# Query projection tiles loaded into gather buffers before the gathers, the first eight expert picks chosen alone, single rows at the end, token tiles loaded first

## Chip, core and metric

One core of one Trainium2 chip runs the whole program. The metric is the device time of one execution in microseconds. Three runs of the kernel before gave 1580.16, 1581.84 and 1583.11 us; their median is 1581.84 us.

## What is computed

Two model blocks run one after the other on 256 tokens of width 1024 (272 rows with the 16 meta rows in the first mixer). The first block is a hybrid mixer followed by a product-key expert layer (PEER). The second block is a retention layer and a stick-breaking attention layer. The change touches the beginning of the first block and its expert layer:

```python
hn = rmsnorm(h, ln_mix_w)                      # h = meta rows and token rows, 272 x 1024
h  = h + hybrid_mixer(hn, ...)                 # ends with  mixed @ w_out
...
q = (hn @ w_q).reshape(n, 8, 2, 128)           # query projection, w_q is 1024 x 2048
s = einsum('nhid,hikd->nhik', q, sub_keys)     # 8 heads x 2 sides x 128 keys
s_top, i_top = top_k(s, 16)                    # per side
cand = s_top[..., 0, :, None] + s_top[..., 1, None, :]
best, pos = top_k(cand, 16)                    # 16 of 256 pairs
idx = key 0 * 128 + key 1 of each pick         # row of the expert tables
w = softmax(best)
act = gelu(einsum('nhkd,nd->nhk', u_tab[idx], hn))
out = einsum('nhk,nhkd->nd', w * act, v_tab[idx])
```

Each token picks 8 x 16 = 128 expert rows, each a row of u and a row of v, 2 x 1024 floats.

## The kernel before

**Weight stream.** All dense weights come as 257 tiles of 128 x 1024 floats (512 KB) in one fixed order, `chunks`. Tile i is loaded by SP (L201) into `raw[i % 4]` by `load` (L210), is split by `do_split` (L215) into a high part (`whi`, ACT, L221) and a low part (`wlo`, DVE, L222) in a ring of five, and is multiplied in three matmuls per product by `triple` (L260). `next_chunk` (L227) splits tile i + 4 when tile i is taken, and each split issues the load of the tile four further on, so a raw buffer is filled again as soon as its split is done. I call the 16 tiles of `peer_w_q` w_q0 to w_q15, and the first tiles after them (retention weights) ret0 to ret3. The output projection takes the eight tiles before w_q0.

**Order by hand.** Each engine runs its own list in program order. Only waits on semaphores tie the lists together. `stream_T` and `stream_N` emit the matmuls of a tile and then one step of a generator in `sides` (`side_step`), so the expert layer's DVE work is laid between the splits: one step of `peer_side` (L1230) after each w_q tile from w_q2 on, and freely once the tiles are out.

**Expert layer.** A pair n = (head, half of the tokens) has 16 picks. `topk(n)` (L1121) finds them on DVE in steps: best 16 of side 0, best 16 of side 1, best 16 of the 256 sums, the table rows (L1134 to L1141), the softmax weights. `gather(m)` (L1176) issues one indirect DMA on POOL (L1187) which brings row m's u and v for 128 tokens, 1 MB, into one of 17 slots; m runs from 0 to 255. Slots 0 to 6 are in the arena AR, 7 and 8 at the upper end of the XH and XL halves of SLAB, 9 is the key table SUBK, 10 to 14 are the `whi`/`wlo` ring and 15 and 16 the rest of XH and XL. `slot_free` (L1159) says what each must wait for on first use: slots 0 to 8 for the output projection, slot 9 for the last scores, slots 10 to 16 for matmuls of the last w_q tiles. Later uses wait for the expert matmul that read the slot's former row. `slot_for` takes the slot that has been held longest.

**Per row.** `dot(m)` (L1196, DVE) multiplies u with HN, the weighted rows made by `weighted_rows` (L1045). `gelu` (L1205, ACT) follows for a group of 4 rows, of 2 from m = 228, of 1 from m = 254. For a group of several, one DVE product (L1210) and a diagonal per row on ACT (L1222); for a single row, one DVE instruction makes the diagonal (L1220). `expert(m)` then does two matmuls with v (L323). The first group's product and matmuls come in the list after dot(10), when the last w_q tile and its scores are out. At m = 243, 245, ... `peer_side` also splits ret0 to ret3.

**Start.** SP loads token tile 0, then the meta rows, which wait until DVE has zeroed their 128 x 1024 tile, then token tile 1, constants C1, parameters PAR and the first four raw tiles. Token tile 1 and the meta rows share a semaphore. Sums of squares (L380 to L382) and `rstd` follow; then per quarter of the width the rows are scaled: meta and tile 0 on DVE (L388, L389), tile 1 on ACT (L390). TensorE transposes them (L326), waiting for C1 and PAR, and L333/L334 split them into XH and XL.

Of the kernel before, what the change touches and what calls it, by code (L numbers as in the profile page):

```python
# [143 lines left out]
def build(nc, stream, par, rows, con1, con2, xin, meta, subk, peer_uv, out, stage=99, debug=None):  # L144
    chunks = chunk_plan()
    ctx = ExitStack()
    with ctx:
# [62 lines left out]
        def load(i):  # L210
            if i < len(chunks) and i == state["load"]:
                state["load"] += 1
                loaded[i] = dma(SP, raw[i % NR][:, :], stream[i], s_raw[i % NR], split.get(i - NR), state["hold"])

        def do_split(i):  # L215

            if i < min(len(chunks), state["limit"]) and i == state["split"]:
# [1641 lines left out]
```

How the kernel before makes its waits and increments, by code:

```python
    def run(self, eng):  # L73
        for waits, make, signal in self.program:
            for sem, value in waits:
                eng.wait_ge(sem, value)
            ins = make(eng)
            if signal:
                ins.then_inc(self.sem, 1)
# [64 lines left out]
def build(nc, stream, par, rows, con1, con2, xin, meta, subk, peer_uv, out, stage=99, debug=None):  # L144
# [55 lines left out]
            def make(e, dst=dst, src=src, s=s):  # L200
                return e.dma_start(dst, src).then_inc(s, 16)
# [974 lines left out]
        def gather(m):  # L1176
# [8 lines left out]
            s = s_uv[j]  # L1185
            dma_count[s.name] = dma_count.get(s.name, 0) + 16
            G(lambda e: e.indirect_dma_start(slots[j], None, peer_uv, bass.IndirectOffsetOnAxis(ap=col, axis=0)).then_inc(s, 16),
              idx_pt[m // 16], free, signal=False, chain=False)
# [535 lines left out]
        A(lambda e: e.activation(SM[:, 30:31], SM[:, 30:31], ACT.Sqrt))  # L1724
        YY = place("YY", 8704, 2048).rearrange("p (i d) -> p i d", i=2)
        stream_N(2, 16, 0, TX, 0, sb_ready, use_y, pick=sb_pick)
        OUT = place("OUT", 10752, 2048).rearrange("p (i d) -> p i d", i=2)
        row_rstd()
        v = post(OUT, False)
        s_out = sem("s_out")
        for (half, i), t in v.items():
            f = slice(512 * half, 512 * half + 512)
            done = dma(SP, out[128 * i:128 * i + 128, f], OUT[:, i, f], s_out, t)
        SP(lambda e: e.wait_ge(*done), signal=False)
        return finish(locals())
```

## Time and profile before

| | us |
|---|---|
| median of three runs | 1581.84 |
| the profiled execution's own time | 1588.28 |
| its span, first to last instruction | 1586.5 |
| PE busy | 1382.9 (87%) |
| PE weight load busy | 992.7 (63%) |
| DVE busy | 1086.4 (68%) |
| ACT busy | 720.7 (45%) |
| POOL busy | 298.5 (19%) |
| mean granted TensorE clock | 0.959 |

The shares are means over stages with different limits. The dense stages (to about 480 us, and from about 1145 us) are filled by PE. Between them lies the expert stage, which moves 268 MB of gathered rows. Times within the span are counted from its first instruction. "Releaser" is what ended an engine's idle time.

### The profile page before, as it was taken

The numbers are of one execution on the slowest core, as the hardware profiler recorded it, in microseconds if no ns is written. First come the engines' busy times: TensorE is split into PE (matmuls) and PEld (weight loads), VectorE is DVE, ScalarE is ACT, GpSimd is POOL, SyncE is SP. The second block draws the span as 40 slices with busy tenths as digits, with TensorE's granted clock in tenths as the row PEclk, the third lists the DMA queues.
The fourth block names the chain that finished last, engine by engine and source line by source line (L and its number), as shares of the span: only waits on it lengthen the run. The fifth ranks groups of instructions, "written<-read, shape, count | busy, mean of one in ns | idle before, by whom it ended". The sixth has DMA issues, their size and how long they took to land. (4 is left out here: it accounts for less than half of the span.)

```text
span 1586.5 us, 19019 instructions
## 1 busy us (share of the span) xinstructions
PE 1382.9 (87%) x6585; PEld 992.7 (63%) x6585; DVE 1086.4 (68%) x2076; ACT 720.7 (45%) x1242; POOL 298.5 (19%) x260
## 2 busy tenths in 40 slices
PE   6999989989999787777877777788799999999997
PEld 5989978968988333333333333333397788998776
DVE  5778578676678777777777677665686466765554
ACT  5666677556454222222222222222454365657772
POOL 0000000000004554443544444442100000000000
PEclk9999999999999898998989999989999999999999
DMA  6453444444559999999999999999655456445442
GB/s 229 125 183 120 161 147 146 140 126 155 178 173 380 418 422 421 421 421 421 422 421 421 422 420 422 421 420 422 271 191 162 124 183 198 158 162 145 147 135 78
DMA packets 77808, 417.73 MB, mean 263 GB/s; under 512 B 8768, under 2 KB 8832, under 8 KB 44688
## 3 DMA queue, kind: packets, MB, share of 16 engines
q0 software_dynamic: 36864, 268.45, 40.7%
q1 hardware_dynamic: 40848, 148.06, 29.4%
q8 instruction: 53, 0.87, 0.2%
q14 instruction: 43, 0.35, 0.1%
HBM read 415.39 MB, written 1.08 MB: 263 GB/s over the span
## 5 line engine op out<-in xcount | busy, mean ns | idle before, releaser
L323 PE MATMUL ps<-AR 128*128 128x512 f32 (+6 forms) x1164 | 365.0, 463 | 103.1 <-ACT AR L1222 74.1
L222 DVE TENSOR_TENSOR wlo<-raw,whi 128x1024 fp32r<-128x1024 f32 x257 | 312.0, 1220 | 159.9 <-ACT whi L221 159.3
L323 PEld LDWEIGHTS ps<-AR 128*128 128x128 f32 (+2 forms) x1164 | 188.9, 194 | 266.6 <-issue 126.6
L221 ACT ACTIVATE whi<-raw 128x1024 fp32r<-128x1024 f32 x257 | 269.2, 1054 | 118.7 <-PE ps L260 95.6
L260 PE MATMUL ps<-XH,whi 128*128 128x256 f32 (+1 forms) x1032 | 305.3, 296 | 9.4 <-DVE XL L334 2.5
L323 PE MATMUL ps<-SLAB,AR 128*128 128x512 f32 x516 | 248.9, 637 | 62.6 <-ACT AR L1222 62.5
L260 PE MATMUL ps<-XL,whi 128*128 128x256 f32 (+1 forms) x1032 | 296.4, 287 | 0.0
L260 PE MATMUL ps<-XH,wlo 128*128 128x256 f32 (+1 forms) x1032 | 296.4, 287 | 0.0
L1187 POOL DMA_INDIRECT AR<-in_peer_uv,C x127 | 148.2, 1167 | 650.0 <-DVE C L1141 475.2
L323 PEld LDWEIGHTS ps<-SLAB,AR 128*128 128x128 f32 x516 | 102.9, 204 | 206.3 <-issue 121.1
L260 PEld LDWEIGHTS ps<-XH,whi 128*128 128x128 f32 x1032 | 199.9, 194 | 19.2 <-issue 6.1
L1196 DVE CUSTOM_DVE_ANT_0 SLAB<-SLAB,AR 128x1024 f32<-128x1024 f32 x129 | 156.8, 1222 | 63.7 <-DMA SLAB<-in_peer_uv,C 63.6
L260 PEld LDWEIGHTS ps<-XL,whi 128*128 128x128 f32 x1032 | 199.9, 194 | 0.7 <-issue 0.5
L260 PEld LDWEIGHTS ps<-XH,wlo 128*128 128x128 f32 x1032 | 199.7, 194 | 0.0
L1196 DVE CUSTOM_DVE_ANT_0 AR<-AR 128x1024 f32<-128x1024 f32 x127 | 154.3, 1222 | 55.2 <-DMA AR<-in_peer_uv,C 54.8
L260 PE MATMUL ps<-whi,XH 128*128 128x512 f32 x448 | 184.9, 413 | 0.0
L1187 POOL DMA_INDIRECT SLAB<-in_peer_uv,C x129 | 150.2, 1164 | 173.8 <-PE ps L323 132.3
L260 PE MATMUL ps<-whi,XL 128*128 128x512 f32 x448 | 176.3, 393 | 0.0
L260 PE MATMUL ps<-wlo,XH 128*128 128x512 f32 x448 | 176.2, 393 | 0.0
L1222 ACT ACTIVATE AR<-C 128x128 f32<-128x128 f32 x254 | 84.4, 392 | 177.3 <-DVE C L1210 150.4
L1205 ACT ACTIVATE C<-C,SM 128x4 f32<-128x4 f32 (+2 forms) x72 | 21.4, 297 | 290.0 <-DVE C L1196 289.8
L260 PEld LDWEIGHTS ps<-whi,XH 128*128 128x128 f32 x448 | 85.2, 190 | 19.5 <-issue 3.2
(251 smaller groups left out, 1219.4 us busy)
## 6 DMA issues: line engine op xcount, KB each, us to landing
raw<-in_stream SPq DMA_DIRECT2D x257, 512.0 KB, 3.9
AR<-scr SPq DMA_DIRECT2D x8, 512.0 KB, 5.4
SLAB<-in_peer_uv,C POOLq DMA_INDIRECT x129, 28.1
AR<-in_rows SPq DMA_DIRECT2D x4, 512.0 KB, 4.7
AR<-in_peer_uv,C POOLq DMA_INDIRECT x127, 27.9
AR<-in_con SPq DMA_DIRECT2D x1, 1280.0 KB, 7.1
AR<-in_xin SPq DMA_DIRECT2D x2, 512.0 KB, 4.9
AR<-in_xin SPq DMA_DIRECT2D x1, 1024.0 KB, 6.1
```

What stands on the lines that cost most here:

```text
L221: a = A(lambda e: e.activation(h[:, :], r, ACT.Copy), loaded[i], free, chain=False)
L222: b = V(lambda e: e.tensor_tensor(l[:, :], r, h[:, :].bitcast(F32), ALU.subtract), a, loaded[i], free, chain=False)
L260: tok = PE(lambda e, s=s, m=m, n=n: e.matmul(out_ap, s, m, start=first and n == 0, stop=last and n == 2), *(after if n == 0 else ()), sign ...
L323: return PE(lambda e: e.matmul(out_ap, l, r, start=start, stop=stop, skip_group_check=onto), *after, signal=sig)
L1187: G(lambda e: e.indirect_dma_start(slots[j], None, peer_uv, bass.IndirectOffsetOnAxis(ap=col, axis=0)).then_inc(s, 16), idx_pt[m // 16], f ...
L1196: dot_pt[m] = V(lambda e: e.tensor_tensor_reduce(u, u, HN[:, i, :], 1.0, 0.0, ALU.mult, ALU.add, AV[:, i, at:at + 1]), uv_in[m], chain=False)
L1205: gelu_pt[ms[0]] = A(lambda e: e.activation(CC[:, i, c], AV[:, i, c], ACT.Gelu_apprx_tanh, scale=SM[:, 24 + i:25 + i]), dot_pt[ms[-1]])
L1222: a = A(lambda e: e.activation(d, ident, ACT.Copy, scale=CC[:, i, c]), c_ready, dg_free.get(m - 4), chain=False)
```

## The change

There are four edits. (1) Eleven of the w_q tiles, w_q4 to w_q14, no longer pass through the four raw buffers. They get homes of their own in gather slots 0, 1, 4, 5, 7 and 8; each is loaded on a semaphore of its own once the matmuls of the SSD up projection (`yt_done`) are over. One of these loads is issued after each split. The raw ring holds the other tiles, so the load which w_q0's split issues is that of w_q15, and the splits of w_q1 to w_q3 issue ret0 to ret2. A slot with a lent tile is offered to `gather` only when the tile's split has been emitted, and waits for it; slot 6, which needs HN, only when HN has been. (2) `topk(0)` finds its best eight pairs, makes their table rows, and only then the other eight. The first gathers are issued between the two, ahead of `weighted_rows`. (3) Groups of one row begin at m = 248 instead of 254. (4) At the start the meta tile is zeroed on POOL, token tile 1 is loaded ahead of the meta rows, with semaphores of their own, and the meta rows are scaled on POOL.

```diff
-        def load(i):
-            if i < len(chunks) and i == state["load"]:
+        first_pq = next(n for n, c in enumerate(chunks) if c[1] == "peer_w_q")
+        high = 2 * NS * CH + 8 * T
+        spare = [(0, AR, 4096), (0, AR, 5120), (4, AR, 20992), (4, AR, 22016), (5, AR, 23040), (5, AR, 24064), (1, AR, 14848),
+                 (7, SLAB, high), (7, SLAB, high + CH), (8, SLAB, high + XW), (8, SLAB, high + XW + CH)]
+        extra = {first_pq + NR + n: buf[:, at:at + CH] for n, (_, buf, at) in enumerate(spare)}
...
+        in_ring = [i for i in range(len(chunks)) if i not in extra]
+        ring_at = {i: n for n, i in enumerate(in_ring)}
+        pending = []
+
+        def load(n):
+            if n < len(in_ring) and n == state["load"]:
...
-                r, h, l = raw[i % NR][:, :], whi[i % NS], wlo[i % NS]
+                r, h, l = extra[i] if i in extra else raw[ring_at[i] % NR][:, :], whi[i % NS], wlo[i % NS]
...
-                load(i + NR)
+                if i in ring_at:
+                    load(ring_at[i] + NR)
+                if pending:
+                    pending.pop(0)()
+
+        def load_ahead(ready):
+
+            for i, tile in extra.items():
+                def make(i=i, tile=tile):
+                    loaded[i] = dma(SP, tile, stream[i], sem(f"s_extra{i}"), ready)
+                pending.append(make)
...
-        z0 = V(lambda e: e.memset(HX[:, 2, :], 0.0))
+        m0 = G(lambda e: e.memset(HX[:, 2, :], 0.0))
         x0_in = dma(SP, HX[:, 0, :], x_tiles[:, 0, :], s_x)
         s_x1 = sem("s_x1")
-        x1_in = dma(SP, HX[0:16, 2, :], meta, s_x1, z0)
+        s_m = sem("s_m")
         x1_in = dma(SP, HX[:, 1, :], x_tiles[:, 1, :], s_x1)
+        meta_in = dma(SP, HX[0:16, 2, :], meta, s_m, m0)
...
-                V(lambda e, f=f: e.tensor_scalar(HX[0:16, 2, f], HX[0:16, 2, f], ss[0:16, 2:3], None, ALU.mult))
+                g = G(lambda e, f=f: e.tensor_scalar(HX[0:16, 2, f], HX[0:16, 2, f], ss[0:16, 2:3], None, ALU.mult), r)
...
-                ready = (ready[1], (v, a)) if c else (None, (v, a))
+                ready = (ready[1], (v, a, g)) if c else (None, (v, a, g))
...
         yt_done = PE.now()
+        load_ahead(yt_done)
...
+            if n == 0:
+                V(lambda e: e.max(BV[:, 0:8], CAND))
+                V(lambda e: e.max_index(idx[:, 0:8], BV[:, 0:8], CAND))
+                early["idx"] = pairs(slice(0, 8))
+                yield
+                V(lambda e: e.match_replace(CAND, BV[:, 0:8], CAND, NEG))
+                V(lambda e: e.max(BV[:, 8:16], CAND))
+                V(lambda e: e.max_index(idx[:, 8:16], BV[:, 8:16], CAND))
+                v = V(lambda e: e.tensor_scalar(SM[:, 28:29], BV[:, 0:1], -1.0, None, ALU.mult))
+                idx_pt[n] = pairs(slice(8, 16))
...
+            if j == 6 and "hn" not in pts:
+                return None
             if j < EARLY:
-                return (pts["hn"], wo_done) if j == 6 else (pts["r"], wo_done, yt_done)
+                tiles = [split.get(i) for i in lent.get(j, ())]
+                if None in tiles:
+                    return None
+                return (pts["hn"], wo_done) if j == 6 else (pts["r"], wo_done, yt_done, tiles)
...
-              idx_pt[m // 16], free, signal=False, chain=False)
+              early["idx"] if m < 8 else idx_pt[m // 16], free, signal=False, chain=False)
...
-            for _ in range(3):
+            for _ in range(2):
                 next(first_topk)
-            weighted_rows()
...
+            while m_next < 8 and gather(m_next):
+                m_next += 1
+            next(first_topk)
+            weighted_rows()
             gathers()
...
-                size = 4 if m < 228 else 2 if m < 254 else 1
+                size = 4 if m < 228 else 2 if m < 248 else 1
```

`pairs(c)` is the former run of seven instructions L1134 to L1141, applied to the picks in the slice c.

## Rows read from the trace of the kernel before

**Rows 1.** Page, part 2: GB/s moved by DMA, in 40 slices of the span.
```profile
GB/s 229 125 183 120 161 147 146 140 126 155 178 173 380 418 422 421 421 421 421 422 421 421 422 420 422 421 420 422 271 191 162 124 183 198 158 162 145 147 135 78
```

**Rows 2.** Windows: stretch, length, five engines' busy us, PE clock, DMA share, GB/s.
```profile
900.00:1080.00 180.00, 137.96 (x279) 57.23 (x280) 126.79 (x307) 40.84 (x107) 79.21 (x69) 0.91 1.01 421
...
534.00:535.00 1.00, 1.00 (x3) 0.40 (x3) 0.00 (x0) 0.40 (x1) 0.31 (x1) 1.00 0.86 295
```

**Rows 3.** Timeline of POOL: start, us, instruction, idle time before it and releaser.
```profile
475.60 2.00 POOL L1187 DMA_INDIRECT AR<-in_peer_uv,C  x1 [475.16 <-DVE C L1141]
...
490.65 0.94 POOL L1187 DMA_INDIRECT SLAB<-in_peer_uv,C  x1 [0.30 <-issue]
506.50 1.10 POOL L1187 DMA_INDIRECT SLAB<-in_peer_uv,C  x1 [14.91 <-PE ps L260]
...
521.35 1.72 POOL L1187 DMA_INDIRECT AR<-in_peer_uv,C  x1 [0.31 <-DVE SM L1131]
531.26 1.36 POOL L1187 DMA_INDIRECT AR<-in_peer_uv,C  x1 [8.19 <-PE ps L323]
```

**Rows 4.** DMA issues from 475.5 to 512 us: count, size, median us to landing.
```profile
raw<-in_stream SPq DMA_DIRECT2D x9, 512.0 KB, 11.9
```

**Rows 5.** Timeline of DVE around the first picks and up to the first group's product.
```profile
469.18 0.43 DVE L1128 TENSOR_TENSOR AR<-AR 128x256 f32<-128x256 f32 x1
...
470.18 0.42 DVE L1116 FIND_INDEX8 AR<-AR 128x8 uint32<-128x256 f32 x1
...
472.34 0.17 DVE L1134 TENSOR_SCALAR AR<-AR 128x16 uint32<-128x16 uint32 x1
...
473.69 0.69 DVE L1139 TENSOR_TENSOR AR<-AR 128x512 f32<-128x512 f32 x1
...
475.14 0.18 DVE L1141 SCALAR_TENSOR_TENSOR C<-AR 128x16 uint32<-128x16 f32 x1
...
477.83 4.62 DVE L222 TENSOR_TENSOR wlo<-raw,whi 128x1024 fp32r<-128x1024 f32 x4
...
488.31 1.23 DVE L222 TENSOR_TENSOR wlo<-raw,whi 128x1024 fp32r<-128x1024 f32 x1 [4.18 <-ACT whi L221]
...
526.70 0.16 DVE L1210 TENSOR_TENSOR C<-C 128x4 f32<-128x4 f32 x1
```

**Rows 6.** Timeline of ACT: the split of w_q11.
```profile
487.22 1.06 ACT L221 ACTIVATE whi<-raw 128x1024 fp32r<-128x1024 f32 x1 [4.59 <-DMA raw<-in_stream]
```

**Rows 7.** Timeline of PE: the first expert matmuls.
```profile
527.35 7.92 PE L323 MATMUL ps<-AR 128*128 128x512 f32 x14 [10.21 <-ACT AR L1222]
```

**Rows 8.** Windows before the gathers, columns as in Rows 2.
```profile
440.00:444.00 4.00, 4.00 (x19) 3.25 (x18) 2.51 (x3) 1.73 (x3) 0.00 (x0) 1.00 0.97 365
...
472.00:476.00 4.00, 4.00 (x36) 4.00 (x35) 3.62 (x10) 2.28 (x4) 0.40 (x1) 1.00 0.01 4
```

**Rows 9.** Landing time of the one raw load issued at 442.6 us (w_q3).
```profile
DMA to landing us min/median/max: 4.6/4.6/4.6
```

**Rows 10.** Timelines of PE and DVE: the last expert rows.
```profile
1137.33 5.42 PE L323 MATMUL ps<-AR 128*128 128x512 f32 x12 [1.25 <-ACT AR L1222]
1142.59 1.88 PE L323 MATMUL ps<-SLAB,AR 128*128 128x512 f32 x4
...
1139.15 1.22 DVE L1196 CUSTOM_DVE_ANT_0 SLAB<-SLAB,AR 128x1024 f32<-128x1024 f32 x1 [0.45 <-DMA SLAB<-in_peer_uv,C]
...
1140.75 0.34 DVE L1220 TENSOR_SCALAR AR<-C 128x128 f32<-128x128 f32 x1 [0.36 <-ACT C L1205]
```

**Rows 11.** Timelines of DVE and PE at the start, and landing of PAR's load issued at 3.3 us.
```profile
1.02 0.91 DVE L365 MEMSET AR<- 128x1024 f32 x1 [1.02 <-PEq L1849]
...
8.25 1.22 DVE L382 CUSTOM_DVE_ANT_0 AR<-AR 128x1024 f32<-128x1024 f32 x1 [5.66 <-DMA AR<-in_xin]
...
11.81 2.82 PE L326 MATMUL ps<-C,AR 128*128 128x128 f32 x12 [11.81 <-DVE AR L389]
...
DMA to landing us min/median/max: 7.9/7.9/7.9
```

More of the change, by code:

```diff
@@ L208, in build @@
         state = {"load": 0, "split": 0, "next": 0, "limit": PEER_END, "fence": None, "hold": None}
-        def load(i):
-            if i < len(chunks) and i == state["load"]:
+        first_pq = next(n for n, c in enumerate(chunks) if c[1] == "peer_w_q")
[3 more added lines that the diff above has]
+        extra = {first_pq + NR + n: buf[:, at:at + CH] for n, (_, buf, at) in enumerate(spare)}
+        lent = {}
+        for n, (j, _, _) in enumerate(spare):
+            lent.setdefault(j, []).append(first_pq + NR + n)
+        in_ring = [i for i in range(len(chunks)) if i not in extra]
[3 more added lines that the diff above has]
+            if n < len(in_ring) and n == state["load"]:
                 state["load"] += 1
-                loaded[i] = dma(SP, raw[i % NR][:, :], stream[i], s_raw[i % NR], split.get(i - NR), state["hold"])
+                i = in_ring[n]
+                loaded[i] = dma(SP, raw[n % NR][:, :], stream[i], s_raw[n % NR], split.get(in_ring[n - NR]) if n >= NR else None,
+                                state["hold"])
         def do_split(i):
@@ L380, in build @@
         a = A(lambda e: e.activation(junk[:, 0, :], HX[:, 0, :], ACT.Square, accum_out=ss[:, 0:1]), x0_in, z0)
-        a = A(lambda e: e.activation(junk[0:16, 0, :], HX[0:16, 2, :], ACT.Square, accum_out=ss[0:16, 2:3]), x1_in)
+        a = A(lambda e: e.activation(junk[0:16, 0, :], HX[0:16, 2, :], ACT.Square, accum_out=ss[0:16, 2:3]), meta_in)
         V(lambda e: e.tensor_tensor_reduce(junk[:, 1, :], HX[:, 1, :], HX[:, 1, :], 1.0, 0.0, ALU.mult, ALU.add, ss[:, 1:2]), x1_in)
@@ L1111, in build @@
         iota16 = C1[:, C_IOTA:C_IOTA + 16]
-        idx_pt, w_pt, c_pt = {}, {}, {}
+        idx_pt, w_pt, c_pt, early = {}, {}, {}, {}
         def best16(vals, idx, src):
@@ L1136, in topk, with pairs @@
-            V(lambda e: e.tensor_copy(AF, AB.bitcast(U32)))
-            V(lambda e: e.tensor_tensor(EQ, AF.unsqueeze(3).broadcast_to([128, 2, 16, 16]),
-                                        iota16.unsqueeze(1).unsqueeze(1).broadcast_to([128, 2, 16, 16]), ALU.is_equal))
-            V(lambda e: e.tensor_tensor(EQ, EQ, TF.unsqueeze(2).broadcast_to([128, 2, 16, 16]), ALU.mult))
-            V(lambda e: e.tensor_reduce(SEL, EQ, AX.X, ALU.add))
-            idx_pt[n] = V(lambda e: e.scalar_tensor_tensor(IDX[:, i, 16 * h:16 * h + 16], SEL[:, 0, :], 128.0, SEL[:, 1, :], ALU.mult,
-                                                           ALU.add))
+            def pairs(c):
+                m = c.stop - c.start
+                eq = EQ[:, :, c, :]
+                V(lambda e: e.tensor_single_scalar(AB[:, 0, c].bitcast(U32), BI[:, c].bitcast(U32), 4, ALU.logical_shift_right))
+                V(lambda e: e.tensor_single_scalar(AB[:, 1, c].bitcast(U32), BI[:, c].bitcast(U32), 15, ALU.bitwise_and))
+                V(lambda e: e.tensor_copy(AF[:, :, c], AB[:, :, c].bitcast(U32)))
+                V(lambda e: e.tensor_tensor(eq, AF[:, :, c].unsqueeze(3).broadcast_to([128, 2, m, 16]),
+                                            iota16.unsqueeze(1).unsqueeze(1).broadcast_to([128, 2, m, 16]), ALU.is_equal))
+                V(lambda e: e.tensor_tensor(eq, eq, TF.unsqueeze(2).broadcast_to([128, 2, m, 16]), ALU.mult))
+                V(lambda e: e.tensor_reduce(SEL[:, :, c], eq, AX.X, ALU.add))
+                return V(lambda e: e.scalar_tensor_tensor(IDX[:, i, 16 * h + c.start:16 * h + c.stop], SEL[:, 0, c], 128.0, SEL[:, 1, c],
+                                                          ALU.mult, ALU.add))
@@ new lines, in topk @@
+            idx = BI.bitcast(U32)
+            if n == 0:
[8 more added lines that the diff above has]
+                idx_pt[n] = pairs(slice(8, 16))
+            else:
+                best16(BV, idx, CAND)
+                v = V(lambda e: e.tensor_scalar(SM[:, 28:29], BV[:, 0:1], -1.0, None, ALU.mult))
+                yield
+                idx_pt[n] = pairs(slice(0, 16))
```

5 lines of the change are left out of this document (removed).

## Prediction

> **What bounds the kernel now.** I read the page's slices first, then windows, then the timelines of the expert stage. The slices show DMA at 421 GB/s from about 480 us to 1110 us and at 120 to 230 GB/s in nearly all other slices [rows 1]. In the windows PE, DVE, ACT and POOL are each well under full while the DMA share is 1.01 [rows 2]. So the expert stage runs at the pace of the transfers, and one gather of 1.049 MB costs 1.049 / 0.421 = 2.49 us. The dense stages on both sides are paced by PE. A us saved ahead of the expert stage, or at its end, comes off the total.
>
> The first reading would be that DMA is the bound from the first gather on, so that every byte taken out of the stage is a gain. POOL's timeline says otherwise. There are 17 slots. The first gather is issued at 475.6 us, the ninth at 490.65, the tenth at 506.5, the 17th at 521.35, and the 18th only at 531.26, after 8.2 us in which POOL waited for an expert matmul [rows 3]. The 18th needs a used slot. Its packets follow its issue by about 2.7 us, so they start near 534. In the window from 534 to 535 us the rate falls to 295 GB/s [rows 2]: the 17 gathers and the loads beside them are just used up then. From there the other 239 gathers run without a gap until the last one lands at 1139.15 us [rows 10], (1139.15 - 534) / 239 = 2.53 us each. The end of the expert stage is the time of the 18th gather plus a fixed 605 us. What counts is what releases the 18th gather.
>
> That is a chain on DVE. The 18th gather waits for expert row 0 on PE, whose matmuls start at 527.35 [rows 7], these for the diagonals on ACT, and these for the first group's product on DVE at 526.70 [rows 5]. In program order this product stands behind the splits of w_q11 to w_q15, dots 0 to 10 and the steps of topk(1) to topk(3). From 488.31 to 526.70 us DVE's timeline has no idle time worth counting. Ahead of it is one hole: the split of w_q11 waits 4.18 us for ACT [rows 5], and ACT waits 4.59 us for w_q11's load [rows 6], which was issued at 479.1, after the first gather.
>
> **Part 1, the tiles loaded ahead.** Nine raw loads (w_q11 to w_q15, ret0 to ret3) are issued between 475.5 and 512 us [rows 4]. In the new order eight of them (all but ret3) are issued before the first gather. That is 8 x 0.524 = 4.19 MB, or 10.0 us of transfer. Only what was waited for comes back: the hole of 4.18 us on DVE. On PE more is saved, since ACT no longer holds up copies behind its waits for loads, but PE is idle for 10.2 us before 527.35 [rows 7], so that saving ends in a longer idle. Value: -4.2 us.
>
> What it adds: gathers 4 to 8 must wait for splits in their slots. Stepping through the lists, gathers 0 to 3 find slots 0, 2, 3 and 6. Gathers 4 to 6 wait on POOL for w_q10's split (about 484 us), gather 7 for w_q12's (about 491), gather 8 for w_q14's (about 501), with gathers 9 and on queued behind it. DMA then runs dry between about 497 and 504 us, and again for some 3 us before the 18th gather. It costs nothing while dots find their rows: dot 8 comes about 12 us after gather 8 is issued, dot 10 about 19 us after gather 10. I take 0, with a bound of 2 us should a row land late.
>
> The doubled loads fall into the output projection: from 436 to 455 us one ring tile and one lent tile per split, 1.05 MB in about 2.8 us or 374 GB/s, against 421 possible. The stretch is not idle now: 365 GB/s from 440 to 444 us, falling to 4 GB/s at 472 to 476 [rows 8]. Behind the key table's load the raw loads would land at intervals of 1.25 us, alternating: w_q3, issued at 442.6, lands after 4.6 us now [rows 9], and with four lent tiles ahead of it at about 447.1 + 3 x 1.25 = 450.9. ACT splits it at 452.2. The smallest slack is about 1.3 us, at w_q2 and w_q3, so I take 0. It is a rival below.
>
> **Part 2, eight picks first.** The seven instructions from 472.34 to 475.32 take 2.98 us; their three long ones take 0.69 each at 512 columns, and 0.43 at 256 columns [rows 5]. For eight picks they take 2.98 - 3 x 0.26 = 2.2 us, and twice that is 4.4, so DVE pays 1.42 us more ahead of HN, the splits of w_q7 to w_q10 and all that follows. The first gather gains: the first index search ends at 470.6, + 2.2 = 472.8, issue at 473.1 instead of 475.6. But an earlier first gather only fills slots sooner; it doesn't move the DVE chain. So this part costs 1.4 us. With part 1 the chain moves by -4.2 + 1.4 = **-2.8 us** (-2.2 to -3.2; 2 us less if a row lands late). PE's w_q7 would wait some 0.1 us for its low part.
>
> **Part 3, single rows from m = 248.** Now rows 252 and 253 wait for each other, PE starts row 252 at 1137.33 and works off four rows to 1144.3 at 1.72 us each [rows 10], though row 255's diagonal is ready at 1141.1. Singly, row 252's dot (ends 1133.0) lets PE start it at 1134.1, row 253 at 1137.0 (a split stands ahead of its diagonal), row 254 at 1139.1 and row 255 at 1141.1, ending at 1142.9. The price on DVE is a wait for gelu of 0.36 and a diagonal of 0.34 per row [rows 10], so two rows with a split take 4.8 us of the 4.98 in which they land. Value: **-1.4 us** (0 to -1.6).
>
> **Part 4, the start.** Token tile 1 lands at 8.2 us [rows 11], 5.9 us after its issue at 2.4. Issued at 1.2 right behind tile 0, which lands at 4.7, it should land at about 6.5. The scaled rows would then be ready 1.7 us sooner, at about 10.0. But the transposes need PAR too, which lands at 3.3 + 7.9 = 11.2, against their start at 11.81 [rows 11]. PAR gains only what the gap in the transfers gives back, up to 0.8 us. So the transposes start 0.6 to 1.4 us earlier, and DVE, rid of four scalings of 0.34 us, gives some 0.4 on the way to the last transpose. POOL's zeroing and scaling are not in the trace (POOL shows no such instruction). DVE takes 0.91 us to zero the tile [rows 11], and from it I bound POOL's between 0.9 and 3 us; at 3 us the meta rows' load, with constants, PAR and raw tiles queued behind it on SP, goes out 1.5 us later, and the gain becomes a loss of about 0.5. Value: **-1.6 us** (+0.5 to -2.3). The Trainium skill (GPSIMD Engine Reference, § 4.1 Engine selection) speaks against the move in general, calling elementwise work on GpSimd about twice as slow with two inputs, but roughly line rate with one; both moved operations have one, and by that rule the sum stays. No run yet shows it.
>
> **Sum.** -2.8 - 1.4 - 1.6 = **-5.8 us**. The profiled execution took 1588.28 us (span 1586.5), 6.4 us above the median of the runs, so it would take 1582.5, and the median goes from 1581.84 to **1576.0 us**. The terms' bounds reach from 1574.7 to 1580.1.
>
> **Rivals.** (a) *The bytes come back one for one.* If DMA and not the chain releases the stage, its saturated stretch loses 10.0 us and starts 2.5 us earlier: 1581.84 - 10.0 - 2.5 - 1.4 - 1.6 = 1566.3 us. For it speaks the full DMA share; against it the 18th gather's wait for PE and the dip at 534. Chance 0.08. The Trainium skill (DMA: Bandwidth & Descriptors, § Queues, rings and completion order) says that each DMA engine takes turns between the queues that have work, so loads and gathers share the rate, which would favour this case; the trace agrees on the sharing (raw loads land after 11.9 us in that stretch [rows 4]), not on what limits the stage.
>
> (b) *Start and tail give nothing, or a row lands late.* POOL is slow or PAR holds the start, and DVE's gelu waits eat the tail's gain, or gather 8's wait holds up dot 8: what is left is about -2.8 us, 1579.0, within 0.2%. Chance 0.20.
>
> (c) *Slower: the doubled loads starve the projections.* If the loads between 436 and 455 us move slower than 374 GB/s, each pair puts the next ring tile later. PE then waits in the output projection and at w_q0 to w_q3, and all behind it is late. It decides once a tile has lost its 1.3 us of slack; at one tile time of 1.25 us for each of eight pairs it costs 10 us: 1576.0 + 10.0 = 1586.0. For it speaks 365 GB/s already at 440 to 444 us [rows 8]; against it, the expert stage's rate of 421. Chance 0.06.
>
> **How the numbers follow.** Forecast 0.66, (a) 0.08, (b) 0.20, (c) 0.06. A measurement of this kernel can tell about 0.2%, or 3.2 us. The forecast's bounds up to 1578.7 are faster by more than that, as is (a), and a quarter of (b): faster 0.79; the rest of (b) within: 0.15; slower 0.06. The range takes in the forecast's bounds and most of (b), and reaches toward (a): 1570.5 to 1580.5.
>
> **What would show it.** Part 1: no wait of ACT for a load in the w_q stage, w_q11's split on DVE right behind dot 0 and its softmax step, no raw load but ret3's between the first gather and 512 us; POOL waiting for ACT or DVE splits before gathers 4, 7 and 8; DMA below full near 500 us. The first group's product 2.8 us nearer to the start of the w_q stage than now, the 18th gather likewise, and the same 605 us after it. Part 2: the first gather 2.5 us earlier against that stage, HN 1.4 us later. Part 3: L1220 eight times, PE's end 3.8 us after the last landing instead of 5.2. Part 4: the first transposes at about 10.5, the first product 1.6 us earlier. It is wrong if the 18th gather follows the transfers and not the first product, or if PE idles between 436 and 460 us.

## The result, and the profile after

| | before | after |
|---|---|---|
| median of five runs, one chip | 1581.99 us | 1575.83 us |
| their range | 1580.16 to 1583.77 | 1574.50 to 1577.61 |
| ratio with 95% interval | | 0.9952 [0.9939, 0.9965] |
| the profiled execution's own time | 1588.28 | 1575.83 |
| its span | 1586.5 | 1574.0 |
| mean granted TensorE clock | 0.959 | 0.964 |

The kernel is faster by 6.2 us or 0.48% (interval 0.35 to 0.61%). It was forecast at 1576.0 us with a gain of 5.8 us. Two rows of the page of after, the engines' one and that of rows 1:

```profile
PE 1377.8 (88%) x6585; PEld 986.6 (63%) x6585; DVE 1086.9 (69%) x2081; ACT 719.0 (46%) x1239; POOL 302.6 (19%) x265
GB/s 231 130 179 121 161 148 139 156 135 161 188 289 324 399 421 420 422 422 421 421 421 421 422 421 422 421 421 421 262 193 165 130 184 193 158 162 145 149 135 80
```

The two profiled executions differ by more than the medians: 12.5 us of span. That has to be sorted out first, or each term would be read too large. The landmark is the first copy out of PSUM at the start of the w_q stage, on ACT; I call it w. From before and then from after, ACT's timeline, and one window of each in the mixer stage (columns as in rows 2):

```profile
461.28 0.37 ACT L1081 COPY AR<-ps 128x256 f32<-128x256 f32 x1
300.00:350.00 50.00, 45.46 (x217) 35.29 (x216) 32.85 (x41) 26.01 (x44) 0.00 (x0) 0.93 0.43 137
```
```profile
454.38 0.37 ACT L1107 COPY AR<-ps 128x256 f32<-128x256 f32 x1
300.00:350.00 50.00, 47.12 (x243) 37.67 (x244) 36.34 (x45) 28.14 (x46) 0.00 (x0) 1.00 0.49 157
```

From the first product to w, a stretch in which only loads were added, before took 461.28 - 19.91 = 441.4 us and after 454.38 - 18.02 = 436.4. The window shows what goes with it: the granted clock was 0.93 in before and 1.00 in after, though the matmuls of the stage are the same. Other profiles speak against an effect of the change. `short_before` below has the code of before in this stretch and took 435.2 us; a second profile of after took 439.7. So 5.0 of the 12.5 us are set aside: what lies ahead of the mixer stage is read from the span's start, and everything behind it is counted from w.

POOL's timeline of after, to be held against rows 3: gathers 1, 4, 5, 8, 9 and 18.

```profile
466.18 1.15 POOL L1236 DMA_INDIRECT AR<-in_peer_uv,C  x1 [452.53 <-ACT AR L1088]
...
472.69 1.68 POOL L1236 DMA_INDIRECT AR<-in_peer_uv,C  x1 [2.71 <-DVE AR L1071]
477.73 1.18 POOL L1236 DMA_INDIRECT AR<-in_peer_uv,C  x1 [3.37 <-ACT AR L1107]
...
484.71 1.17 POOL L1236 DMA_INDIRECT SLAB<-in_peer_uv,C  x1 [2.88 <-DVE wlo L236]
494.57 1.17 POOL L1236 DMA_INDIRECT SLAB<-in_peer_uv,C  x1 [8.69 <-ACT AR L1088]
...
521.64 1.22 POOL L1236 DMA_INDIRECT AR<-in_peer_uv,C  x1 [11.43 <-PE ps L347]
```

DVE's timeline of after, to be held against rows 5: both instructions of `weighted_rows`, the splits of w_q7 to w_q10, the softmax step after dot 0, w_q11's split, and the first group's product.

```profile
469.94 2.49 DVE L1071 TENSOR_TENSOR AR<-AR 128x1024 f32<-128x1024 f32 x2
472.34 4.62 DVE L236 TENSOR_TENSOR wlo<-AR,whi 128x1024 fp32r<-128x1024 f32 x4
...
478.41 0.23 DVE L1190 TENSOR_SCALAR C<-C,SM 128x16 f32<-128x16 f32 x1
478.55 1.22 DVE L236 TENSOR_TENSOR wlo<-SLAB,whi 128x1024 fp32r<-128x1024 f32 x1
...
516.94 0.16 DVE L1259 TENSOR_TENSOR C<-C 128x4 f32<-128x4 f32 x1
```

The hole of 4.18 us in front of w_q11's split [rows 5] is gone: the split starts at 478.55 directly behind the softmax step, with no idle time noted. The first group's product comes 516.94 - 454.38 = 62.6 us after w, where before had 526.70 - 461.28 = 65.4. The 18th gather still waits for an expert matmul, now for 11.43 us.

The transfers of after, in windows with the columns of rows 2:

```profile
492.00:496.00 4.00, 4.00 (x36) 4.00 (x35) 3.83 (x10) 3.10 (x7) 1.17 (x1) 1.00 0.00 2
...
508.00:512.00 4.00, 0.00 (x0) 0.00 (x0) 3.72 (x14) 0.00 (x0) 1.91 (x2) 0.50 1.02 424
...
522.00:523.00 1.00, 1.00 (x3) 0.47 (x2) 0.96 (x4) 0.40 (x1) 0.86 (x1) 0.50 0.28 115
523.00:524.00 1.00, 1.00 (x3) 0.40 (x2) 0.40 (x2) 0.00 (x0) 0.00 (x0) 0.79 0.86 123
524.00:525.00 1.00, 1.00 (x4) 0.52 (x3) 0.00 (x0) 0.40 (x1) 0.56 (x1) 1.00 0.55 180
```

They fall to 2 GB/s while the ninth gather waits for its slot, run at 424 again, and dip just before the 18th gather's packets arrive. I call the size of that dip D. It is the time that the transfers lose against 421 GB/s in the 20 us from 8 us ahead of the 18th gather's issue to 12 us behind it: 20 x (421 - rate) / 421. These windows of before, of after and of `lent7`, an experiment below:

```profile
523.26:543.26 20.00, 15.91 (x33) 7.02 (x34) 10.98 (x23) 7.87 (x18) 8.27 (x7) 0.81 1.01 416
```
```profile
513.64:533.64 20.00, 16.05 (x31) 7.08 (x32) 10.05 (x22) 7.65 (x17) 7.00 (x7) 0.76 0.94 375
```
```profile
513.60:533.60 20.00, 15.81 (x33) 7.01 (x34) 11.07 (x23) 7.86 (x18) 8.41 (x7) 0.82 0.83 323
```

D is 2.2 us in after, 4.7 in lent7, and only 0.2 in before, where the window of 295 GB/s [rows 2] is the one low one and some of its neighbours lie above 421. The depth of this dip will matter more than anything else below.

The tail, PE's and DVE's timelines of after, to be held against rows 10:

```profile
1130.68 1.98 PE L347 MATMUL ps<-SLAB,AR 128*128 128x512 f32 x4 [0.20 <-DVE AR L1269]
1132.50 1.94 PE L350 MATMUL ps<-C,AR 128*128 128x128 f32 x16
...
1128.68 1.23 DVE L1245 CUSTOM_DVE_ANT_0 SLAB<-SLAB,AR 128x1024 f32<-128x1024 f32 x1 [0.24 <-DMA SLAB<-in_peer_uv,C]
...
1130.28 0.35 DVE L1269 TENSOR_SCALAR AR<-C 128x128 f32<-128x128 f32 x1 [0.36 <-ACT C L1254]
```

The transposes that follow the last row start 3.8 us after the last landing, against 5.2 us in before, from 1139.15 [rows 10] to this row of its PE timeline:

```profile
1144.31 1.94 PE L326 MATMUL ps<-C,AR 128*128 128x128 f32 x16
```

Without the mixer stage the profiled difference is 7.5 us: 1.9 at the start, 3.6 from w to the last landing, 1.3 in the tail and 0.7 behind it. The medians say 6.2.

### The profile page after: what moved, and what is told of

The parts are those of the page before. It is cut to its first block and busy times, and to the rows that moved or that the text cites. A ratio compares the mean times of both kernels' runs of the same rounds, so it can differ in the third digit from the quotient of the medians.

```text
span 1574.0 us, 19025 instructions
## 1 busy us (share of the span) xinstructions
PE 1377.8 (88%) x6585; PEld 986.6 (63%) x6585; DVE 1086.9 (69%) x2081; ACT 719.0 (46%) x1239; POOL 302.6 (19%) x265
## 3 DMA queue, kind: packets, MB, share of 16 engines
HBM read 415.39 MB, written 1.08 MB: 265 GB/s over the span
## 5 line engine op out<-in xcount | busy, mean ns | idle before, releaser
L347 PE MATMUL ps<-AR 128*128 128x512 f32 (+6 forms) x1164 | 369.2, 466 | 98.1 <-ACT AR L1271 71.6
L236 DVE TENSOR_TENSOR wlo<-raw,whi 128x1024 fp32r<-128x1024 f32 x246 | 298.6, 1221 | 150.5 <-ACT whi L235 149.8
L235 ACT ACTIVATE whi<-raw 128x1024 fp32r<-128x1024 f32 x246 | 257.5, 1054 | 100.7 <-PE ps L284 90.3
L347 PE MATMUL ps<-SLAB,AR 128*128 128x512 f32 x516 | 244.0, 627 | 62.1 <-ACT AR L1271 61.9
```

The costliest lines, as they stand in the source:

```text
L235: a = A(lambda e: e.activation(h[:, :], r, ACT.Copy), loaded[i], free, chain=False)
L236: b = V(lambda e: e.tensor_tensor(l[:, :], r, h[:, :].bitcast(F32), ALU.subtract), a, loaded[i], free, chain=False)
L347: return PE(lambda e: e.matmul(out_ap, l, r, start=start, stop=stop, skip_group_check=onto), *after, signal=sig)
```

## The experiments

Two theories stood against each other. The chain theory: the 18th gather follows DVE's chain, and the bytes taken out of the gather stage are worth nothing by themselves. The transfer theory, rival (a): the stage takes as long as its bytes, and each 421 KB are worth 1 us. The table gives for each profile, in us, P (the first group's product), G (the 18th gather's issue) and L (the last landing, by the start of the last dot), all counted from w, then L - G and D; then the median and the ratio to the kernel before in the same session. Lines with the same session number share a chip and its runs of before.

| kernel | P | G | L | L - G | D | median, us | ratio to before | session |
|---|---|---|---|---|---|---|---|---|
| before | 65.4 | 70.0 | 677.9 | 607.9 | 0.2 | 1581.99 | 1 | 0 |
| after | 62.6 | 67.3 | 674.3 | 607.0 | 2.2 | 1575.83 | 0.9952 [0.9939, 0.9965] | 0 |
| no_lent | 67.1 | 71.8 | 679.4 | 607.6 | 1.5 | 1579.86 | 0.9985 [0.9974, 0.9996] | 1 |
| no_early8 | 61.5 | 66.2 | 674.0 | 607.8 | 2.8 | 1572.94 | 0.9951 [0.9936, 0.9966] | 1 |
| no_tail | 62.6 | 66.9 | 674.6 | 607.6 | 2.6 | 1579.06 | 0.9977 [0.9967, 0.9987] | 1 |
| no_start | 62.9 | 67.6 | 674.7 | 607.2 | 2.5 | 1577.84 | 0.9969 [0.9957, 0.9980] | 1 |
| short_before | 60.2 | 64.9 | 677.8 | 612.9 | 0 | 1581.14 | 0.9992 [0.9980, 1.0004] | 2 |
| short_after | 56.2 | 60.9 | 672.1 | 611.2 | 0 | 1573.90 | 0.9943 [0.9925, 0.9961] | 2 |
| bytes_back | 63.5 | 68.2 | 675.8 | 607.6 | 0.7 | 1578.39 | 0.9960 [0.9946, 0.9974] | 2 |
| lent7_short | 56.2 | 60.9 | 669.8 | 608.9 | 0 | 1571.53 | 0.9925 [0.9907, 0.9942] | 2 |
| after_again | 62.5 | 66.8 | 674.5 | 607.7 | 2.4 | 1574.68 | 0.9960 [0.9946, 0.9974] | 3 |
| lent7 | 62.5 | 67.0 | 674.7 | 607.7 | 4.7 | 1575.21 | 0.9957 [0.9945, 0.9969] | 3 |
| lent7_short_again | 56.2 | 60.9 | 670.0 | 609.2 | 0 | 1571.26 | 0.9926 [0.9912, 0.9941] | 3 |

P repeats within 0.1 us in two profiles of one kernel (62.56 and 62.54; 56.19 and 56.15), G and L within 0.4. That is far finer than the medians, so the marks carry the argument and the ratios check it.

**Undo part 1 (no_lent).** No tile is lent, all else as in after.

```diff
-        spare = [(0, AR, 4096), (0, AR, 5120), (4, AR, 20992), (4, AR, 22016), (5, AR, 23040), (5, AR, 24064), (1, AR, 14848),
-                 (7, SLAB, high), (7, SLAB, high + CH), (8, SLAB, high + XW), (8, SLAB, high + XW + CH)]
+        spare = []
```

> The changed kernel without its first part: no tile has a home in a gather slot, all pass through the four raw buffers again. Chain theory (the 18th gather follows the first group's product on DVE): the hole before w_q11's split is back, 4 to 5.5 us, so the first product comes 4 to 5.5 us later against the w_q stage than in the changed kernel, and the time is about 1576 + 5 = 1581 us, 1 us below the kernel before, since start and tail still give 3.2 us and the second part costs DVE 1.4 us. Bytes theory (the transfers set the end of the expert stage): 10 us of loads are back in the stage, 1576 + 10 = 1586 us.

ACT's and DVE's timelines of no_lent, w_q11's split on both:

```profile
484.96 1.06 ACT L234 ACTIVATE whi<-raw 128x1024 fp32r<-128x1024 f32 x1 [5.34 <-DMA raw<-in_stream]
...
486.05 1.23 DVE L235 TENSOR_TENSOR wlo<-raw,whi 128x1024 fp32r<-128x1024 f32 x1 [4.30 <-ACT whi L234]
```

The hole is back with its cause: ACT waits for the load, DVE for ACT. P is 4.6 us later than in after, G 4.6, L 5.1. The time loses most of the change's gain: 0.9985 against 0.9952. Where the transfer theory wanted 1586 us, it is 1579.86. This kernel also gives the price of part 2 under the old chain: P is 67.1 - 65.4 = 1.7 us later than in before.

**Undo part 2 (no_early8).** `topk(0)` runs through as in before, `weighted_rows()` and the gathers follow.

```diff
-            if n == 0:
+            if n < 0:
...
-              early["idx"] if m < 8 else idx_pt[m // 16], free, signal=False, chain=False)
+              idx_pt[m // 16], free, signal=False, chain=False)
...
-            for _ in range(2):
+            for _ in range(3):
                 next(first_topk)
+            weighted_rows()
...
-            while m_next < 8 and gather(m_next):
-                m_next += 1
-            next(first_topk)
-            weighted_rows()
             gathers()
```

> The changed kernel without its second part: topk(0) chooses all 16 picks at once and the gathers come behind HN. Chain theory: DVE is spared 1.4 us ahead of the w_q7 split, so the first product and the 18th gather come 1.4 us earlier and the time is 1576 - 1.4 = 1574.6 us, although the first gather is issued 2.5 us later. Theory that the first gather sets the stage: 1576 + 2.5 = 1578.5 us.

P moved by 1.1 us and G by 0.7 to 1.1, but L by only 0.3 against after and 0.6 against after_again, and the ratio stayed (0.9951). The first gather was issued 14.3 us behind w instead of 11.8. So the part costs 1.1 to 1.7 us in the chain, as its instructions say. How much of that reaches the end stays open between 0.3 and 1: L scatters by 0.4 between profiles and the ratios by more. The earlier first gather has bought nothing visible: undone, D is 2.8, not smaller than the 2.2 of after.

**Undo part 3 (no_tail).**

```diff
-                size = 4 if m < 228 else 2 if m < 248 else 1
+                size = 4 if m < 228 else 2 if m < 254 else 1
```

> The changed kernel with groups of two rows up to m = 253 again. If the tail gave what the prediction says: PE ends its last expert row 5.2 us after the last landing instead of 3.8, and the time is 1576 + 1.4 = 1577.4 us. Rival (DVE's waits for gelu ate it): no change, 1576 us.

PE's and DVE's timelines of no_tail, the end of the gather stage:

```profile
1129.92 5.42 PE L347 MATMUL ps<-AR 128*128 128x512 f32 x12 [1.24 <-ACT AR L1271]
...
1131.74 1.23 DVE L1245 CUSTOM_DVE_ANT_0 SLAB<-SLAB,AR 128x1024 f32<-128x1024 f32 x1 [0.44 <-DMA SLAB<-in_peer_uv,C]
...
1136.90 0.27 PE L350 MATMUL ps<-C,AR 128*128 128x128 f32 x1
```

PE again works off 12 matmuls in one piece while the last row is already there; the transposes start at 1136.90, 5.2 us behind the landing. The mark says 1.34 us. The ratio is 0.0025 above that of after, 4 us, with intervals of 0.0010 and 0.0013 to either side, and 0.0017 above that of after_again; it confirms the sign and is too coarse for the size.

**Undo part 4 (no_start).**

```diff
-        m0 = G(lambda e: e.memset(HX[:, 2, :], 0.0))
+        z0 = V(lambda e: e.memset(HX[:, 2, :], 0.0))
...
+        x1_in = dma(SP, HX[0:16, 2, :], meta, s_x1, z0)
         x1_in = dma(SP, HX[:, 1, :], x_tiles[:, 1, :], s_x1)
-        meta_in = dma(SP, HX[0:16, 2, :], meta, s_m, m0)
...
-        a = A(lambda e: e.activation(junk[0:16, 0, :], HX[0:16, 2, :], ACT.Square, accum_out=ss[0:16, 2:3]), meta_in)
+        a = A(lambda e: e.activation(junk[0:16, 0, :], HX[0:16, 2, :], ACT.Square, accum_out=ss[0:16, 2:3]), x1_in)
...
-                g = G(lambda e, f=f: e.tensor_scalar(HX[0:16, 2, f], HX[0:16, 2, f], ss[0:16, 2:3], None, ALU.mult), r)
+                V(lambda e, f=f: e.tensor_scalar(HX[0:16, 2, f], HX[0:16, 2, f], ss[0:16, 2:3], None, ALU.mult))
...
-                ready = (ready[1], (v, a, g)) if c else (None, (v, a, g))
+                ready = (ready[1], (v, a)) if c else (None, (v, a))
```

> The changed kernel with the start of the kernel before: the meta tile zeroed on DVE, meta rows loaded ahead of token tile 1, meta rows scaled on DVE. If the start gave what the prediction says, the first product of the first stage comes at 19.9 us instead of 18.0 and the time is 1576 + 1.9 = 1577.9 us. Rival (the start is covered by the loads of the first weight tiles): no change, 1576 us.

The first product, PE's timeline of no_start and then of after:

```profile
19.86 0.57 PE L284 MATMUL ps<-XH,whi 128*128 128x272 f32 x1
```
```profile
18.02 0.37 PE L284 MATMUL ps<-XH,whi 128*128 128x272 f32 x1
```

They are 1.84 us apart. But the old start is not the same each time. From PE's timelines, the first transposes of short_before (whose start is before's), and of after:

```profile
10.89 2.82 PE L326 MATMUL ps<-C,AR 128*128 128x128 f32 x12 [10.89 <-DVE AR L389]
```
```profile
10.89 2.79 PE L350 MATMUL ps<-C,AR 128*128 128x128 f32 x12 [10.89 <-POOL AR L413]
```

In short_before token tile 1 happened to land at 7.3 us instead of 8.2, and the first transposes then start at 10.89, as in after. Its first product still came at 18.98, 1.0 us later than in after. The three profiles with the old start give 19.91, 19.86 and 18.98 us, the ten with the new one (after among them) 17.8 to 18.4. By this mark the part is worth 1.5 to 2.1 us in the usual case and 0.6 to 1.2 when the old order is lucky. After is one of four profiles in which the mark came 0.6 us early for another reason; part 4 below takes that apart.

**Is it the bytes? (bytes_back).** After, with eight transfers of 512 KB added in the gather stage, one behind each of the splits of w_q7 to w_q14. They copy weight tiles to a scratch tensor that nobody reads, so the 4.19 MB that part 1 took out of the stage are moved there again, and nothing waits for them.

```diff
+        spill = nc.dram_tensor("spill", [8, 128, CH], F32).ap()
...
+                if first_pq + 7 <= i < first_pq + 15:
+                    n = i - first_pq - 7
+                    dma(SP, spill[n], stream[n], sem(f"s_spill{n}"), split[i])
```

> The changed kernel with eight more transfers of 512 KB from the weight stream into a scratch tensor in device memory, which nobody reads, issued after the splits of w_q7 to w_q14, so behind the first gathers. They put back the bytes that the change took out of the stage, but nobody waits for them. Bytes theory: 8 x 1.25 = 10 us, 1586 us. Chain with the transfers as second bound: the gaps before the 18th gather (some 8 us between 480 and 504 us and 2 us at 522) take most of them, 1576 to 1578.5 us.

The DMA issues of bytes_back, columns as in rows 4, and POOL's 18th gather:

```profile
spill<-in_stream SPq DMA_DIRECT2D x8, 512.0 KB, 7.6
```
```profile
522.76 1.21 POOL L1240 DMA_INDIRECT AR<-in_peer_uv,C  x1 [11.43 <-PE ps L351]
```

The 10.0 us of transfers cost 0.9 us at P and 1.2 to 1.5 us at L, and the ratio is 0.9960 [0.9946, 0.9974]. The transfer theory wanted 10 us; one for one it falls. Where the other 8.5 us went, the window from 20 us behind w to 8 us ahead of the 18th gather shows, in after and then in bytes_back:

```profile
474.38:513.64 39.26, 30.07 (x252) 29.69 (x250) 37.14 (x97) 16.19 (x31) 14.37 (x13) 0.91 0.86 329
```
```profile
474.60:514.76 40.16, 30.16 (x252) 29.76 (x251) 37.25 (x97) 16.21 (x31) 15.70 (x13) 0.91 1.01 404
```

In after the transfers lose 8.6 us against 421 GB/s there, since the gathers wait for splits in their slots. In bytes_back they lose 1.6: the added ones have filled 7.0 us. The other 1.5 us go into the dip, where D shrinks from 2.2 to 0.7. So they are cheap, but most of the reserve is used up with them.

**Lend less (lent7).** Only the seven lent tiles in the arena stay; the four in slots 7 and 8 go back to the raw ring, and four loads with them behind the first gather. This undoes the waits of POOL for splits in these slots.

```diff
-        spare = [(0, AR, 4096), (0, AR, 5120), (4, AR, 20992), (4, AR, 22016), (5, AR, 23040), (5, AR, 24064), (1, AR, 14848),
-                 (7, SLAB, high), (7, SLAB, high + CH), (8, SLAB, high + XW), (8, SLAB, high + XW + CH)]
+        spare = [(0, AR, 4096), (0, AR, 5120), (4, AR, 20992), (4, AR, 22016), (5, AR, 23040), (5, AR, 24064), (1, AR, 14848)]
```

> The changed kernel with seven lent tiles instead of eleven and nothing else: slots 7 and 8 lend none, so gathers 7 and 8 go out earlier, and the loads of w_q15 and ret0 to ret2 fall among the gathers again. The chain on DVE is the same. Chain theory: the first product stays at 62.6 us behind the first copy of the w_q stage, the 18th gather is issued at 67.3 and lands at 73.2 as in the changed kernel, and the time is the same, 1576 us, although the 17th gather lands 2 us earlier. Bytes theory: four loads back in the stage, 1576 + 5 = 1581 us. Theory that gaps in the transfers cost time by themselves: up to 5 us faster, 1571 us.

POOL's timeline of lent7, the ninth and tenth gathers:

```profile
481.10 0.94 POOL L1235 DMA_INDIRECT AR<-in_peer_uv,C  x1 [0.30 <-issue]
...
494.28 1.68 POOL L1235 DMA_INDIRECT SLAB<-in_peer_uv,C  x1 [12.24 <-PE ps L283]
```

The ninth is issued at 481.10 us, 26.5 us behind w instead of 40.2, and the long wait moves to the tenth. P, G and L agree with after_again within 0.2 us, and the ratios with each other (0.9957 and 0.9960). Four loads more in the stage cost nothing, and neither did the waits for splits. What does change is D: 4.7 us instead of 2.4, since the earlier gathers use DMA where it stood idle in after.

**Shorten the chain in the kernel before (short_before) and in after (short_after).** Two steps of a later `topk` that stand behind rows 8 and 9, ahead of the first group's product, move to rows 25 and 26.

```diff
-                if m < 24 or m % 3 == 0:
+                if m not in (8, 9) and (m < 27 or m % 3 == 0):
```

> The kernel before with the same two topk steps moved behind the first product. There the 17th gather lands at 536.0 and the 18th at 538.5, one gather apart, so the transfers have no gap to give back. Chain theory alone: 1582 - 6.5 = 1575.5 us. Chain with the transfers as second bound: no change, 1582 us, with the 18th gather issued 6.5 us earlier and landing when it did.

> The changed kernel with two steps of topk moved behind the first group's product on DVE (the steps after dots 8 and 9, 6.5 us of DVE work). The first product and the issue of the 18th gather come 6.5 us earlier against the w_q stage. Chain theory alone: the last landing comes 6.5 us earlier too, 1576 - 6.5 = 1569.5 us. Chain with the transfers as second bound: the 18th gather can land at the earliest one gather (2.5 us) after the 17th, which lands at 523.7 in the changed kernel against 527.6 for the 18th, so only 1.4 us come back: 1574.6 us.

DVE's product, POOL's 18th gather and the window behind it, in short_before:

```profile
514.34 0.16 DVE L1210 TENSOR_TENSOR C<-C 128x4 f32<-128x4 f32 x1
...
519.05 0.93 POOL L1187 DMA_INDIRECT AR<-in_peer_uv,C  x1 [3.90 <-PE ps L323]
```
```profile
520.00:524.00 4.00, 4.00 (x11) 1.76 (x10) 3.39 (x6) 0.80 (x2) 1.84 (x2) 1.00 1.02 424
```

Here is a second bound. In short_before P and G come 5.2 and 5.1 us earlier, not the 6.5 expected, since DVE then waits 1.2 us for row 10 to land. Yet L stays (677.8 against 677.9), and the time is that of before (0.9992 [0.9980, 1.0004]). The window tells why: 424 GB/s and no dip. The 17 gathers and the raw loads are still moving when the 18th gather joins them, its issue has stopped mattering, and L - G, 607.0 to 607.9 wherever there is a dip, grows to 612.9. In short_after P comes 6.4 us earlier than in after, L only 2.2 to 2.5, and D goes from 2.2 (2.4 in after_again) to 0. In both pairs L gains what the dip held and no more: 0.1 of 0.2, and 2.2 to 2.5 of 2.2 to 2.4.

**Move the second bound as well (lent7_short, lent7_short_again).** If the transfers now decide, starting them earlier should pay: lent7 issues the ninth gather 13.7 us earlier. Its edit and that of short_after together.

> The changed kernel with the two topk steps moved, and with only seven lent tiles (slots 7 and 8 lend none): w_q11 to w_q14 are loaded early through the raw ring instead, and w_q15 and ret0 to ret2 fall among the gathers again. Gathers 7 and 8 no longer wait for splits, so the gaps of the transfers near 482, 494 and 503 us should be filled. Summed from the first landing: 16 gathers of 2.49 us, five tiles of 1.25 and 0.6 for the tables put the 17th landing 5.2 us earlier against the w_q stage, and the 18th 6.5 us earlier: 1576 - 6.5 = 1569.5 us. Bytes theory as in the prediction's rival (loads in the stage cost what they move): four tiles are back, 1576 + 5 = 1581 us. Chain alone: 1569.5 us as well.

> Seven lent tiles and the two topk steps moved, once more, beside the changed kernel on the same chip: 4.5 us less than it from the first copy of the w_q stage to the last landing, so 1571.5 us if the changed kernel takes 1576.

L came to 669.8 and 670.0: 4.7 to 4.9 us ahead of lent7, whose dip held 4.7, and 2.1 to 2.3 ahead of short_after, although four more loads run in the stage. The ratios are 0.9925 [0.9907, 0.9942] and 0.9926 [0.9912, 0.9941] on two chips. In the last session this kernel's median is 3.4 us below after's (1571.26 and 1574.68). It is the best of the study and beats both kernels. The 6.5 us that I expected of L against after were too many by 2: D is 0 and L - G is 609, so 1.3 us or more of the chain's gain meet the transfers' bound again.

**The same kernel twice (after_again).** After, in the session of lent7.

> The changed kernel as it is, beside the next two on one chip, so that they can be compared with it directly: 0.995 of the kernel before, 1575 to 1576 us.

0.9960 [0.9946, 0.9974], against 0.9952 in the first session.

## Why the prediction was right

| term | forecast | shown, and by what |
|---|---|---|
| hole ahead of w_q11 | -4.2 | -4.6 at P, no_lent |
| eight picks first | +1.4 | +1.7 at P (no_lent against before), +1.1 (no_early8) |
| both, at the first group's product | -2.8 | -2.9 |
| tail | -1.4 | -1.3, no_tail |
| start | -1.6 | -1.9 in the profile, 0.6 of it not shown to be part 4's; -1.3 to -1.7 without that |
| sum | -5.8 | -6.1 by these marks, -5.5 without the 0.6; -6.2 by the medians |

**The bound.** The step on which all rested was that the 18th gather, not the bytes, sets the end of the stage. In after it does. no_lent moves the chain back by 4.6 us and the end by 5.1; bytes_back moves 10 us of transfers back and the end by 1.5 at most. The fixed stretch was forecast at 605 us from the gather's first packets. Counted from its issue it is 607.0 to 607.9 in before, in after and in the seven experiments with a dip.

**Where the step was too strong.** The prediction took the window of 295 GB/s as proof that transfers run dry in before, and left its depth unread. The dip is 0.2 us: the two bounds were level, and short_before shows it, where 5.2 us off the chain bring 0.1. A chain shortened by 2.8 us alone would have met the transfers' bound almost at once. That the -2.8 counts in full was luck as far as the working goes, since the change also moves the transfers' bound, in two ways that the sum valued at nothing: part 1 takes 10 us of transfers out of the stage, and part 2 starts the gathers 2.5 us earlier.

Either seems to be enough. Without the second (no_early8) L is no later than in after. Without the first (bytes_back) it is still 2.1 us earlier than in before, with the same bytes to move. Both lines run from 11.8 us behind w to the last landing, of before and then of bytes_back:

```profile
DMA packets 38477, 274.29 MB, mean 412 GB/s; under 512 B 4272, under 2 KB 4272, under 8 KB 5680
```
```profile
DMA packets 37581, 274.29 MB, mean 413 GB/s; under 512 B 4272, under 2 KB 4272, under 8 KB 4656
```

At 421 GB/s both need 651.5 us, so before lost 14.6 us there and bytes_back 12.4. The largest single difference is in the first 8 us of the stretch, where the later first gather left before at 118 GB/s and bytes_back ran at 251: 2.5 us less lost. In no_early8 the same late start (122 GB/s) is made up behind it, because less is lost in the gaps that follow: 4.9 us between 20 us behind w and 8 us ahead of the 18th gather, against 8.6 in after. No run changed the first gather alone in before, so its worth there is read from this account and not tested.

**Part 1, the side costs.** The waits of POOL came where forecast (before gathers 5, 8 and 9, counted from one), and so did the idle DMA: 497 to 504 us was forecast on before's clock, 36 to 43 us behind w, and the window of 2 GB/s is 38 to 42 us behind it. Taken at 0, they measured 0 (lent7 removes the one before the ninth and gains nothing). Rival (c) is judged under the output projection, by windows of before and then of after, both from 26.3 or 26.4 us ahead of w:

```profile
435.00:455.00 20.00, 20.00 (x93) 16.37 (x92) 12.88 (x15) 10.15 (x16) 0.00 (x0) 1.00 0.74 252
```
```profile
428.00:448.00 20.00, 20.00 (x93) 16.36 (x92) 12.89 (x15) 10.23 (x15) 0.00 (x0) 1.00 0.97 366
```

PE is busy throughout and does the same 93 matmuls in both, and from the end of these windows to w neither idles more than 0.8 us. The doubled loads cost PE nothing. They moved at 371 to 417 GB/s in the windows of 4 us from 436 to 456, one of them (444 to 448) a little below the 374 at which rival (c) set in; it did no harm. Rival (c) is out.

**Part 2.** Right in sign and place, at 1.1 to 1.7 us for 1.4. The 2.5 us of the earlier first gather came exactly (11.8 us behind w against 14.3) and, as forecast, don't move the chain.

**Part 3.** The sum of the gelu wait and the diagonal per row held: 0.36 and 0.35 us in after, and DVE was in time for the last row, which it started 0.24 us after its landing.

**Part 4.** The two steps of the gain came as forecast, though POOL, whose prices were open, now sets the first. From the start of after, POOL's and DVE's timelines:

```profile
0.74 0.95 POOL L389 MEMSET AR<- 128x1024 f32 x1 [0.29 <-POOLq L1901]
...
6.66 1.22 DVE L407 CUSTOM_DVE_ANT_0 AR<-AR 128x1024 f32<-128x1024 f32 x1 [5.26 <-DMA AR<-in_xin]
...
9.55 4.10 POOL L413 TENSOR_SCALAR AR<-AR,SM 16x256 f32<-16x256 f32 x4 [7.86 <-DVE SM L381]
```

The zeroing took 0.95 us, at the lower end of the range of 0.9 to 3. Tile 1 landed at 6.66 us (forecast 6.5). But the four small scalings took 0.91 to 1.08 us each, 4.10 in all, where DVE takes 0.34 for one: POOL kept DVE's pace in the large instruction and not in the small ones. The first transposes now wait for POOL, at 10.89 in after and at 10.49 to 10.89 in the ten profiles with this start, for the forecast 10.5. The last six transposes ahead of the first product, in before, after and after_again:

```profile
18.71 1.54 PE L326 MATMUL ps<-C,AR 128*128 128x128 f32 x6 [2.60 <-DVE AR L389]
```
```profile
17.39 0.87 PE L350 MATMUL ps<-C,AR 128*128 128x128 f32 x6 [2.17 <-DVE AR L414]
```
```profile
16.98 1.54 PE L350 MATMUL ps<-C,AR 128*128 128x128 f32 x6 [1.94 <-DVE AR L414]
```

From the first transposes to these it takes 6.9 us with the old start and 6.5 with the new one, in every profile: that is the forecast 0.4 of DVE, rid of the scalings. With the 0.9 to 1.3 us ahead of it, part 4 is worth 1.3 to 1.7 us. The rest of after's 1.9 lies behind: PE went from these transposes to the first product in 0.6 us in after and three other profiles, all with the new start, and in 1.2 in the other nine, after_again among them, whose product came at 18.18. Nothing on record shows why, so these 0.6 us are not shown to be the change's work.

**Rivals.** (a) is out by its own number, 1566.3, and by bytes_back. (b), 1579.0, is out by the time; of its mishaps only POOL's slowness showed, and the first transposes came at most 0.4 us later than forecast. The remaining 0.7 us of the profiled -3.6 between w and L are the difference of L - G, 607.9 against 607.0. after_again has 607.7, so it is scatter of single profiles rather than a gain.

## What to carry to other kernels

A stage can move its bytes at full rate and still be set by one chain of another engine, if slots limit what may be outstanding: look for the first transfer that needs a used slot, for what releases it, and for a dip in the rate just before it. Measure that dip: a shorter chain is worth what the dip holds (0.2, 2.2 to 2.4 and 4.7 us here gave 0.1, 2.2 to 2.5 and 4.7 to 4.9) and no more, so move transfers and chain together. When two profiles differ by more than the medians, find a landmark behind the stretch whose clock differs and count from there.

## What the runs showed of the hardware

**A last DMA engine lags.** Windows of before and then of after, in the last us of the gather stage, columns as in rows 2:

```profile
1132.00:1136.00 4.00, 3.62 (x8) 1.44 (x8) 2.83 (x5) 1.86 (x4) 0.00 (x0) 1.00 0.08 31
```
```profile
1122.00:1124.00 2.00, 2.00 (x5) 0.71 (x5) 1.43 (x4) 1.14 (x2) 0.00 (x0) 1.00 0.08 33
```

From 1122 us on the DMA share of after is 0.08, about one engine of 16, and the last row lands only at 1128.7. In the trace's packet records the last 8 KB packets of the stage, over some 6 us, follow one another without overlap, 0.31 us each, in before as in after: one engine is still at work and the others have nothing left. That it fell behind little by little over some 240 gathers, by about 1% of their 605 us, would explain it, but isn't shown, and what makes it slower wasn't tried. An even share would be worth up to some 5 us by estimate, nearly as much as the whole change.

**The clock of the mixer stage.** From the first product to w, the thirteen profiles range from 434.3 to 441.4 us, on the same matmuls. In the five longest (439.1 us and more) the mean granted clock from 200 to 400 us is 0.95 or 0.96, in the eight others 0.96 to 0.98. Which of the two brings about the other isn't shown.

**The clock after a pause.** In after's windows PE has no matmul from 508 to 512 us, and the granted clock is 0.50, the lower of its two levels (1.2 GHz). Expert matmuls run from 517 on, and the clock is still 0.50 from 522 to 523 and full only from 524 on. The matmuls that release the 18th gather thus run at the lower level. In before they do too: the clock is 0.50 from 524 to 530. From the first group's product to the 18th gather it is 4.6 us in before and 4.7 in after, so the change moved nothing here. What the lower level costs wasn't measured by itself.
